# Order of the first weight panel and the rows x at the start of a one-core decoder step

## The reference

```python
h = rmsnorm(x, norm_pre_mix)
q_f, k_f, v_f, f_logit, q_d, k_d, v_d = split(h @ w_in)        # w_in: 2048 x 7688
o_fox = forgetting attention of 8 heads; the samples also read 2048 cached keys and values through a page table
o_dil = dilated window attention of 3 groups x 4 heads
gates = sigmoid(h @ w_gate + b_gate)
m = (g_fox * (o_fox @ w_o_fox) + g_dil * (o_dil @ w_o_dil)) @ w_out
x = x + rmsnorm(m, norm_post_mix)
y = x + rmsnorm(swiglu(rmsnorm(x, norm_pre_ffn), w_gate_up, w_down), norm_post_ffn)
```

## Time and profile before

| | us |
|---|---|
| median of 3 runs | 2564.36 (2563.03 to 2570.11) |
| the profiled execution, its own time | 2567.03 |
| its span | 2565.4 |
| mean granted clock of TensorE | 0.969 of full |

### The profile page before, as it was taken

How to read it: one execution, slowest core, us unless ns; L and a number is a source line. 1 busy time by engine, 2 the same in 40 slices (tenths; PEclk the granted TensorE clock), 3 DMA queues, 4 the chain that set the end, 5 groups by cost and what they waited for, 6 DMA issues and landing times.

```text
span 2565.4 us, 45356 instructions
## 1 busy us (share of the span) xinstructions
PE 2372.6 (92%) x18306; PEld 2153.3 (84%) x18306; DVE 1024.8 (40%) x1359; ACT 856.5 (33%) x985; POOL 417.3 (16%) x852
## 2 busy tenths in 40 slices
PE   7999999997899998998888986999999999899996
PEld 6999999996666666666588965999999999899995
DVE  6443434333333333333255344333333333344444
ACT  3223233232333324333222233433343343233322
POOL 2010000002333323333210000111111111122210
PEclk8999999998999999999999998999999999899998
DMA  8454344536999999999756433767676776688871
GB/s 248 152 160 153 118 127 154 182 100 202 325 324 350 370 318 306 348 368 339 275 187 209 150 112 106 252 219 246 228 242 231 243 236 220 200 262 274 288 264 47
DMA packets 338964, 585.73 MB, mean 228 GB/s; under 512 B 20431, under 2 KB 282899, under 8 KB 334831
## 3 DMA queue, kind: packets, MB, share of 16 engines
q0 software_dynamic: 70704, 309.02, 34.2%
q1 hardware_dynamic: 268128, 274.86, 33.9%
HBM read 564.06 MB, written 109.39 MB: 263 GB/s over the span
## 4 chain that ended last, share of the span: by engine, by line
PE 77%; DMA 10%; DVE 4%; issue 4%; ACT 3%; POOL 1%; POOLq 0%; SPq 0%; DVEq 0%; ACTq 0%
PE ps L762 14%; PE ps L763 14%; PE ps L764 14%; DMA kraw<-in_cache_fox_k 5%; PE ps L807 5%; PE ps L809 5%; PE ps L808 5%; PE ps L996 3%; PE ps L1001 2%; PE ps L1021 2%; PE ps L985 1%; PE ps L1081 1%; PE ps L986 1%; PE ps L987 1%; DMA kraw<-in_cache_win_k 1%
## 5 line engine op out<-in xcount | busy, mean ns | idle before, releaser
L1485 DVE TENSOR_TENSOR w_lo<-raw,w_hi 128x2048 fp32r<-128x2048 f32 (+2 forms) x250 | 524.2, 2097 | 970.2 <-ACT w_hi L1199 970.2
L1199 ACT ACTIVATE w_hi<-raw 128x2048 fp32r<-128x2048 f32 (+2 forms) x250 | 439.2, 1757 | 927.8 <-PE ps L764 640.8
L762 PE MATMUL ps<-act_hi,w_hi 128*128 128x320 f32 x1664 | 516.0, 310 | 29.4 <-DVE act_lo L1514 22.5
L763 PE MATMUL ps<-act_lo,w_hi 128*128 128x320 f32 x1664 | 515.6, 310 | 0.0
L764 PE MATMUL ps<-act_hi,w_lo 128*128 128x320 f32 x1664 | 515.5, 310 | 0.0
L762 PEld LDWEIGHTS ps<-act_hi,w_hi 128*128 128x128 f32 x1664 | 313.5, 188 | 30.1 <-issue 30.1
L807 PE MATMUL ps<-act_hi,w_hi 128*128 128x320 f32 x1024 | 323.2, 316 | 3.3 <-DVE v_stage L1607 3.3
L809 PE MATMUL ps<-act_hi,w_lo 128*128 128x320 f32 x1024 | 317.2, 310 | 0.0
L808 PE MATMUL ps<-act_lo,w_hi 128*128 128x320 f32 x1024 | 317.1, 310 | 0.0
L763 PEld LDWEIGHTS ps<-act_lo,w_hi 128*128 128x128 f32 x1664 | 313.6, 188 | 0.0
L764 PEld LDWEIGHTS ps<-act_hi,w_lo 128*128 128x128 f32 x1664 | 313.5, 188 | 0.0
(11 more groups left out here) (339 smaller groups left out, 3663.6 us busy)
## 6 DMA issues: line engine op xcount, KB each, us to landing
raw<-in_w_gate_up SPq DMA_DIRECT2D x88, 1024.0 KB, 6.5
kraw<-in_cache_fox_k POOLq DMA_DIRECT2D x128, 512.0 KB, 6.9
vraw<-in_cache_fox_v POOLq DMA_DIRECT2D x128, 512.0 KB, 7.2
raw<-in_w_in SPq DMA_DIRECT2D x60, 1024.0 KB, 7.8
raw<-in_w_gate SPq DMA_DIRECT2D x32, 1024.0 KB, 14.1
raw<-in_w_down SPq DMA_DIRECT2D x32, 1024.0 KB, 6.1
out_win_k_sample<-in_cache_win_k POOLq DMA_DIRECT2D x64, 510.0 KB, 5.9
out_win_v_sample<-in_cache_win_v POOLq DMA_DIRECT2D x64, 510.0 KB, 4.1
```

The lines of the kernel that those rows point to most:

```text
L762: pe.matmul(ps[:, bk_, 0:T], w_hi[:, slot, k, :], xh[:, x_k, :], start=(k == k0), stop=False)
L763: pe.matmul(ps[:, bk_, 0:T], w_hi[:, slot, k, :], xl[:, x_k, :], start=False, stop=False)
L1199: act.activation(w_hi[:, slot, 0:kt, :], raw[:, pslot, 0:kt, P * slot:P * slot + P], ACT.Copy).then_inc(hi_done, 1)
L1485: dve.tensor_tensor(w_lo[:, slot, 0:kt, :], raw[:, pslot, 0:kt, P * half:P * half + P], w_hi[:, slot, 0:kt, :].bitcast(F32), ALU.subtract) ...
```

## The change

The two loads of panel 0 are moved ahead of x in SP's queue. The two splits on ACT are moved ahead of the squares of x, and those on DVE ahead of its copies of x. The quarters then run without a split between them. SP's loop begins with panel 1.

```diff
@@ block.sync
             sp.dma_start(ident[:], I["shape_consts"][:, C_ID:C_ID + P]).then_inc(in_id, 16)
+            first = kblocks(w_in)
+            sp.dma_start(raw[:, 0, 0:8, :], first[:, 0:8, 0:256]).then_inc(raw_ld[0], 16)
+            sp.dma_start(raw[:, 0, 8:KT, :], first[:, 8:KT, 0:256]).then_inc(raw_ld[0], 16)
             xp = I["x_prompt"][0].rearrange("(t p) d -> p t d", p=P)
...
-            for p in range(U_O // 2):
+            for p in range(1, U_O // 2):
@@ block.scalar
             act.activation(stat[0:1, 15:16], ones[0:1, 0:1], ACT.Sqrt)
+            split_hi(0, 0, 32)
+            split_hi(1, 0, 32)
             for t in range(3):
...
-            split_hi(0, 0, 32)
-            first_high(0)
-            split_hi(1, 0, 32)
-            for q in range(1, 4):
+            for q in range(4):
                 first_high(q)
@@ block.vector
+            split_lo(0, 0, 0)
+            split_lo(1, 0, 1)
             for t in range(3):
                 rows = P if t < 2 else NS
                 for q in (0, 2, 3):
...
-            first_normed(0)
-            split_lo(0, 0, 0)
-            first_low(0)
-            first_normed(1)
-            split_lo(1, 0, 1)
-            first_low(1)
-            for q in (2, 3):
+            for q in range(4):
                 first_normed(q)
                 first_low(q)
```

## The result

The changed kernel takes 2572.03 us (median of 20 runs, 2563.48 to 2577.87), the kernel before 2566.28 (20 runs, 2560.74 to 2574.38). The ratio is 1.0020, with a 95% interval of 1.0011 to 1.0030: 5.1 us more (2.8 to 7.7), where 4.7 were forecast. (The two medians by themselves are 5.75 apart.) The change does not pay. It costs about 0.2%: too little for three runs, which differ by 7 us among themselves, but the 20 runs of each kernel tell it from nothing.

What follows compares the result with a forecast made beforehand. TensorE is busy almost throughout, so only the start counts, bound by DVE from 18.11 us; normalising +7.3 and quarters -2.6 give +4.7 us, median 2564.4 to 2569.1 us, range 2563.5 to 2575.5.

Steps and rivals of the forecast that it cites:

- The panel's landing: First panel's two loads, queued first, are in at 10.9 us in place of 19.1; bounds 9.4 and 12.
- x behind it: Loads queued after the panel: x tile 0 lands about 13.8 us, sample rows at 18.2, constants at 19.1.
- the first rival: SP's issue of x and constants is held up, slower by over 0.3%; constants at 26 give +9.2 us; chance 0.07.
- The statistics: On DVE, after splits and nine copies of x, they start at about 22.3 us in place of 15.03.
- This is the step that costs: DVE's nine copies of x queue behind its splits, ending at 22.0 us; normalising starts 7.3 us later.
- The third rival: x is hardly later because engines share time among queued loads; still +4.7 us, or +3.2 with panel at 9.4; chance 0.06.
- From the statistics to normalising: The old 3.08 us stays, so the first normalising on DVE starts at 25.4 us.
- The quarters: Four DVE quarters without splits take 4.7 us each, 18.8 in place of 21.4: 2.6 us saved.
- TensorE: Its matmuls in the quarters, partly at half rate, add nothing; bounds -0.5 and +3.5 us.
- Other queues: POOL's store of xT and picks go out 3 us later, but both are covered, at no cost.
- To the end: Later work is released by TensorE's progress, so the front's +4.7 us shift passes through to the end.

Runs made afterwards that it cites:

- e1: Kernel before with only panel 0's loads moved ahead of x in SP's queue, splits left in the quarters; 2571.41 us, ratio 1.0024 to the kernel before.
- e3: Changed kernel with GpSimd's store of xT held until the three diagonals are done; 2571.16 us, ratio 1.0026 to the kernel before.
- e4: Changed kernel plus matmuls of no use on TensorE, 4 after the transposes and 14 before the first quarter; 2570.75 us, ratio 1.0019 to the kernel before.
- e2: Kernel before with only ACT's and DVE's splits moved ahead of squares and copies, x still first in the queue; 2581.41 us, ratio 1.0064.
- e5: Kernel before with DVE's ntmp of the next quarter ahead of act_lo of the last, ACT's act_hi(1) before a split; 2567.71 us, ratio 1.0005.
- e9: Kernel before with DVE's next ntmp ahead of the last act_lo and TensorE taking unit 1 one quarter earlier; 2563.02 us, ratio 0.9992.
- e8: Changed kernel with DVE's quarters reordered, matmuls of no use, TensorE's unit 1 a quarter earlier, GpSimd's store held until the diagonals; 2564.64 us, ratio 1.0003.

## Why the prediction was right, step by step

- **The panel's landing.** 10.9 forecast by the pair that found its queue empty; measured 1.92 + 7.8 = 9.7, inside the bounds of 9.4 and 12 but near the low one. Data began a little sooner than for x before: 137 GB/s in 3.0 to 3.5 us, where there were 33.
- **x behind it.** x tile 0 at 12.3 (13.8 forecast), the sample rows at 17.5 (18.2 forecast), the constants at 18.5 (19.1). The reasoning by the same total of bytes held to 0.7 for what comes last; tile 0 was 1.5 early. The issue of x was held up once, for 1.44 us at 2.54, with no more than the panel's two halves ahead of it, where the first rival reckoned with a hold-up from some 2.5 halves on. There was no gap in the transfers, so that rival did not come about.
- **The statistics.** 22.3 forecast, 20.85 measured: 1.45 too late, 1.1 of it from the panel. And the reason was wrong. "This is the step that costs" put the loss on DVE's copies behind the splits. e1 took the splits away and the statistics started at 20.77. Two limits coincide here, the copies behind the splits (16.11 to 20.78, without a gap) and the copies behind the transposes of late x; the second alone is enough. The third rival, x not late, was priced as if the first limit stood alone; no run tried it with the panel early as well.
- **From the statistics to normalising.** 3.08 taken over from before, 4.53 measured: 1.45 too little. This is the other error's size, so by luck 25.38 came out as 25.4. The diagonals took 1.36 and not 0.68, because now GpSimd's store is issued in the same moment (e3 shows it); the six matmuls behind them took 1.81 and not 1.04, at half rate, which differs between executions and is not shown to come from the change. I moved the release of POOL by 3 us in the prediction and looked only for what waits for it, not for what runs beside it.
- **The quarters.** 18.8 forecast, 25.38 to 44.19 are 18.8.
- **TensorE.** No cost forecast, none measured, by a hair (from the last act_lo to the bias matmuls 5.53, before 5.55). All matmuls from 30.30 to 39.6 ran at half rate, the granted clock was 0.50 in 24 to 30 and in 30 to 37; e4 shows that full rate there gains nothing; the third quarter's were done at 44.03 + 0.31, and the last started at 44.25. Bias matmuls 49.72, forecast 49.8.
- **Other queues.** No wait for picks or for the store of xT, as forecast.
- **To the end.** The shift passes, by e2, by the table and by the times: measured +5.1 (2.8 to 7.7) for +4.62 in the front. The times of e5 to e9 are too coarse to tell how much of a shift of 2 to 4 us passes.

The median came out 3 us above the forecast, 2572.0 against 2569.1: 1.9 of that is the kernel before, whose 20 runs have their median at 2566.3 and not at the 2564.4 of the first three.

## What to carry to other kernels

Where the transfers at the start fill the DMA engines, the queue order only hands out lateness: put first what has the longest chain behind it (here x, with squares, transposes, root and four quarters), not what the chain of waits happens to end on. Then look at the order on the engine that the chain runs through; here a reordering of DVE's and TensorE's work brought the front some 3 us forward by the traces, which the transfers could not; in the time it is 2 to 3 us, at the edge of what 12 runs can tell. And compare landmarks along two traces, not their spans: here a 4.6 us shift was hidden by a stage that differs by up to 12 us between executions.

## What the runs showed of the hardware

- Three instructions on DVE (tensor_scalar, 128x128, float32) took 0.68 us by themselves and 1.36 or 1.37 in the changed kernel, e1, e2 and e4, where GpSimd issued a 1.33 us DMA of 2.5 MB from 0.01 us after their start. With that issue moved behind them (e3, e8) they took 0.68. No other instruction of DVE in the start showed it.
- The same 32 transposes of x took 3.36, 4.89 and 5.33 us (changed, e4, e2), at 272 ns each to begin with in the first and 421 in the other two. The clock column says 1.00 for all of e4's; ahead of the first change that the trace records, the durations tell the rate and the column does not.
- After TensorE's idle time of 5.48 us before 30.3 it stayed at half rate for 9.3 us, over 30 matmuls with a gap of 1.05 between; before the change the 24 matmuls behind the second quarter had full rate from 30.25 to 31.5, half rate to 34.7, and full rate from then on.
